# Order of transfers and weight splits around the start of an attention block: last weights sliced per head, first keys fetched in the third group, v of two heads split first

## The reference, cut to what matters

```
h = rms_norm(x)
c_q, c_kv, k_rope, z = split(h @ w_in)          # widths 768, 256, 32, 1024
q  = (rms_norm(c_q)  @ w_uq )  -> 16 heads x 96
kv = (rms_norm(c_kv) @ w_ukv)  -> 16 heads x (64 of k, 64 of v)
q, k = rope(rms_norm per head)
o = softmax(causal(q k^T / sqrt(96))) v
x = x + (o * silu(z)) @ w_out                   # the last product
```

## Time and profile before

| | us |
|---|---|
| three timed runs | 1054.29, 1054.57, 1055.83 |
| median | 1054.57 |
| the profiled execution | 1054.33 |
| its span | 1052.5 |
| PE busy | 1016.8 (97%) |
| PE weight loads busy | 845.5 (80%) |
| DVE busy | 611.9 (58%) |
| ACT busy | 464.8 (44%) |
| POOL busy | 226.8 (22%) |
| mean granted TensorE clock | 0.989 of full speed |

### The profile page before, as it was taken

The page is one execution under the profiler, slowest core; times in us unless marked ns, Lnnn a source line. Parts: engine busy times, 40 slices in busy tenths (PEclk is TensorE's granted clock), DMA queues, the critical chain, the costliest instruction groups (busy, mean ns, idle before and its releaser), DMA issues. The chain is left out here.

```text
span 1052.5 us, 15593 instructions
## 1 busy us (share of the span) xinstructions
PE 1016.8 (97%) x5979; PEld 845.5 (80%) x5979; DVE 611.9 (58%) x1111; ACT 464.8 (44%) x868; POOL 226.8 (22%) x397
## 2 busy tenths in 40 slices
PE   5999999999999999999999999998899999997998
PEld 4888888888888888888888999886677787776887
DVE  5653555436634443312453789977699999996221
ACT  6301111111223223322234766757699999997000
POOL 0000000000000002200001579884863333321000
PEclk9999999999999999999999999999899999998999
DMA  9300211211324332312102145485955444521222
GB/s 279 54 22 21 61 40 40 60 40 51 110 100 149 131 140 54 112 40 61 40 21 80 61 170 196 169 209 169 224 149 133 86 94 88 99 41 61 100 90 70
DMA packets 166427, 103.11 MB, mean 98 GB/s; under 512 B 76497, under 2 KB 150737, under 8 KB 166097
## 3 DMA queue, kind: packets, MB, share of 16 engines
q1 hardware_dynamic: 159280, 101.73, 34.3%
q10 hardware_dynamic: 7072, 0.39, 0.5%
HBM read 55.96 MB, written 29.36 MB: 81 GB/s over the span
## 5 line engine op out<-in xcount | busy, mean ns | idle before, releaser
L106 PE MATMUL banks<-front_act_hi,front_w_hi 128*128 128x512 f32 x608 | 239.9, 395 | 10.7 <-DVE front_w_lo L525 10.7
L108 PE MATMUL banks<-front_act_hi,front_w_lo 128*128 128x512 f32 x608 | 238.1, 392 | 0.0
L107 PE MATMUL banks<-front_act_lo,front_w_hi 128*128 128x512 f32 x608 | 237.9, 391 | 0.0
L106 PEld LDWEIGHTS banks<-front_act_hi,front_w_hi 128*128 128x128 f32 x608 | 115.1, 189 | 36.7 <-issue 8.7
L107 PEld LDWEIGHTS banks<-front_act_lo,front_w_hi 128*128 128x128 f32 x608 | 115.0, 189 | 24.2 <-issue 0.5
L108 PEld LDWEIGHTS banks<-front_act_hi,front_w_lo 128*128 128x128 f32 x608 | 114.9, 189 | 24.0
L374 POOL TENSOR_TENSOR front_sq<-front_sq,front_squares 128x1024 f32<-128x1024 f32 x6 | 14.4, 2397 | 450.5 <-ACT front_squares L487 450.5
L392 ACT ACTIVATE front_w_hi<-front_w 128x1024 fp32r<-128x1024 f32 x43 | 45.6, 1060 | 148.2 <-DMA front_w<-in_w_in_ab 103.1
L1418 DVE TENSOR_TENSOR heads_pt_lo<-banks,heads_pt_hi 128x512 f16<-128x512 f32 (+2 forms) x192 | 102.2, 554 | 14.1 <-ACT heads_pt_hi L1309 9.5
L1309 ACT ACTIVATE heads_pt_hi<-banks 128x512 f16<-128x512 f32 (+2 forms) x192 | 89.2, 486 | 18.7 <-PE banks L1577 18.6
L1595 PE MATMUL banks<-heads_v,heads_pt_hi 128*128 128x128 f16 x576 | 75.9, 222 | 2.8 <-POOL heads_v L1514 1.9
(11 more groups left out here) (246 smaller groups left out, 2070.5 us busy)
## 6 DMA issues: line engine op xcount, KB each, us to landing
qk_scratch<-heads_y SPq DMA_DIRECT2D x32, 512.0 KB, 3.3
front_w<-in_w_in_ab SPq DMA_DIRECT2D x21, 512.0 KB, 3.9
front_w<-in_w_in_c SPq DMA_DIRECT2D x17, 512.0 KB, 4.1
y<-in_x_t SPq DMA_DIRECT2D x8, 512.0 KB, 8.1
front_w<-in_w_out_ab SPq DMA_DIRECT2D x8, 512.0 KB, 4.0
front_x<-in_x_t SPq DMA_DIRECT2D x8, 512.0 KB, 5.2
x_scratch<-front_x SPq DMA_DIRECT2D x8, 512.0 KB, 4.0
v_scratch<-heads_v SPq DMA_DIRECT2D x32, 128.0 KB, 3.0
```

The source lines that it names most:

```text
L106: nc.tensor.matmul(out, w_hi, a_hi, start=first, stop=False)
L107: nc.tensor.matmul(out, w_hi, a_lo, start=False, stop=False)
L108: return nc.tensor.matmul(out, w_lo, a_hi, start=False, stop=last)
```

## The change

Four edits, none of which adds or removes arithmetic.

1. Table `when`: the splits of the next group's weights move from t = 2, 3, 4, 5, 6 with 3, 2, 1, 1, 1 chunks to t = 3, 4, 5, 6 with 1, 2, 2, 3.
2. Transposing loads of k and q are issued apart. k of head 0 is loaded in the third group (t = 1), q of head 0 there at t = 3; k and q of head 1 in the fourth group at t = 1 and t = 3, v of heads 0 and 1 at t = 5. The wait for group 0's stores moves to the third group, the wait for the end of group 2's products stays ahead of head 1's k.
3. The 8 slices of `w_out` are no longer issued in a row after the last unit. One goes behind the q and k of each head 4 to 11.
4. GpSimd splits v of head 1 directly behind that of head 0, ahead of `finish(28)`.

```diff
-    when = {2: chunks[0:3], 3: chunks[3:5], 4: chunks[5:6], 5: chunks[6:7], 6: chunks[7:8]}
+    when = {3: chunks[0:1], 4: chunks[1:3], 5: chunks[3:5], 6: chunks[5:8]}
...
-        def load_qk(h):
-            e, first = h % 2, slice(h * BLK, (h + 1) * BLK)
-            sp.dma_start_transpose(k_t[e][:], qk_d[:, 1, first]).then_inc(qk_in[e], 16)
-            sp.dma_start_transpose(q_t[e][:], qk_d[:, 0, first]).then_inc(qk_in[e], 16)
+        def load_k(h):
+            sp.dma_start_transpose(k_t[h % 2][:], qk_d[:, 1, h * BLK:(h + 1) * BLK]).then_inc(qk_in[h % 2], 16)
+
+        def load_q(h):
+            sp.dma_start_transpose(q_t[h % 2][:], qk_d[:, 0, h * BLK:(h + 1) * BLK]).then_inc(qk_in[h % 2], 16)
...
-            if t == 0 and g == G - 1:
+            if g == G - 2 and t == 1:
                 group_stored(0)
+                load_k(0)
+            if g == G - 2 and t == 3:
+                load_q(0)
+            if g == G - 1 and t == 1:
                 sp.wait_ge(q_ready, (G - 1) * NT)
-            if g == G - 1 and t in (0, 2):
-                load_qk(t // 2)
-            if g == G - 1 and t == 4:
+                load_k(1)
+            if g == G - 1 and t == 3:
+                load_q(1)
+            if g == G - 1 and t == 5:
                 load_v(0)
...
         sp.wait_ge(q_ready, UNITS)
-        for m in range(NK):
-            sp.dma_start(w_next[:, m], w_out.rearrange("(k p) c -> p k c", p=P)[:, :, m * P:(m + 1) * P]
-                         ).then_inc(w_next_in, 16)
         for h in range(2, HEADS):
             if h % HPG == 0:
                 group_stored(h // HPG)
             sp.wait_ge(s_ready, NT * (h - 1))
-            load_qk(h)
+            load_k(h)
+            load_q(h)
+            if 0 <= h - HPG < NK:
+                m = h - HPG
+                sp.dma_start(w_next[:, m], w_out.rearrange("(k p) c -> p k c", p=P)[:, :, m * P:(m + 1) * P]
+                             ).then_inc(w_next_in, 16)
             if h % 2 == 0:
                 sp.wait_ge(v_low, h)
                 load_v(h)
...
         split_v(0)
+        split_v(1)
         finish(LATE)
         for h in range(HEADS):
-            if h + 1 < HEADS:
+            if 1 < h + 1 < HEADS:
                 split_v(h + 1)
```

## The result

The changed kernel takes 1049.14 us in the median of five runs (1047.12 to 1051.10). Five runs of the kernel before beside them have a median of 1055.26. The ratio is 0.9941, with a 95% interval of 0.9924 to 0.9958: faster by 6.1 us. The forecast was 1044.8 with a range up to 1049.0, so the direction was right, the gain was 6.1 in place of 9.6, and the time fell just outside. The profiled execution took 1049.57, its span 1047.8, 4.7 less than before.

A forecast was written before the change was run, and what follows sets the result against it. TensorE, busy 97% of the span, bounds the kernel; only idle and low-clock stretches can yield time. Attention start 2.3 us plus heads 1 and 2 7.3 us, 9.6 off, gave 1044.8 us, own range 1043 to 1046.5, wider range 1041.2 to 1049.

The forecast's parts named there:

- v of head 1 first, head 2's q in time: Heads 1 and 2: TensorE's waits of 1.95 and 2.95 us go with their slow stretches, gaining 7.3 us.
- The bound of 15.5: Head 1: VectorE is busy 15.54 us in its window, so it can't come under 15.5 us.
- One sign: Heads 1 and 2: the granted clock between them was to be 1.00.
- the fourth rival: Heads 1 and 2: only one wait goes with its slow stretch, 3.3 us; 1051.1 us, chance 0.05.
- The slices, one per head: Heads 4 to 11: one w_out transfer behind each head's q delays no later load; cost taken as nothing.
- Head 1's k and q in the fourth group: Fourth group: with one pair of loads, the store goes out earlier and the attention's start moves up by 2.6 us.
- Head 0's k in the third group: Third group: its load behind the weights delays a store; ScalarE waits 0 to 4 us, TensorE 0 to 1.5.
- The second rival: Third group: k of head 0 delays a store and gives back the fourth group's gain; 1047.1 us, chance 0.15.
- The weight splits: Third group: first split at t = 3 removes ScalarE's 2.86 us landing wait; with head 0's loads, taken as -0.3 us.
- the sign of this: Third group: the forecast is wrong if TensorE waits over 2 us near 662 or near 678.
- The margin of 0.24 us: Splits at t = 6: the last ended at 679.50, TensorE read it at 679.74; zero to 0.6 us of waiting expected.
- The rule that I quoted: SyncE's queue: a transposing load behind a burst of weights waits for the burst, and the store behind it for both.

The follow-up runs named there:

- experiment 2: Kernel before with two edits alone, w_out sliced per head and v of head 1 split right behind that of head 0: 1045.23 us, ratio 0.9911.
- Experiment 8: Kernel before with v of head 1 split first, alone: 1055.16 us, ratio 1.0003.
- experiment 4: Kernel before with only the loads of k and q of heads 0 and 1 and of v moved as in the change: 1052.86 us, ratio 0.9982.
- experiment 1: Changed kernel with the old table of weight splits: 1044.06 us, ratio 0.9902 against the kernel before.
- experiment 3: Kernel before with the new table of weight splits alone: 1060.61 us, ratio 1.0050.
- experiment 6: Changed kernel, new table kept, each group's weights issued in parts of 2, 3 and 3 behind three units' stores, two units earlier: 1043.28 us, ratio 0.9897.
- experiment 7: Kernel before with w_out sliced per head alone: 1047.46 us, ratio 0.9934.

## Why the prediction was wrong, by its own steps

**v of head 1 first, head 2's q in time: right.** Neither wait is left. Head 1 takes 14.96 us (forecast 15.5), head 2 13.11. The gain is 7.86 against 7.3. The bound of 15.5 was a wrong reading. VectorE's 15.54 us were those of a window of 21.19 us, and some of that work was already head 2's: 15 low parts of the probabilities, where head 1's own window has 12, in the changed kernel as in experiment 2. The roots in it are the same in both.

```profile
L1418 DVE TENSOR_TENSOR heads_pt_lo<-banks,heads_pt_hi 128x512 f16<-128x512 f32 (+3 forms) x15 | 7.8, 545 | 3.0 <-ACT heads_pt_hi L1309 3.0
...
L1426 DVE TENSOR_TENSOR heads_pt_lo<-banks,heads_pt_hi 128x512 f16<-128x512 f32 (+3 forms) x12 | 6.3, 553 | 0.5 <-ACT heads_pt_hi L1317 0.2
```

VectorE is busy 13.63 us in head 1 now, and head 1 takes 14.69 in experiment 2. So the number came out near by some luck. One sign was missed: the clock between the two waits was to be 1.00, and it is 0.89 in head 1, where the slow stretch of the start now lies. Experiment 8 adds what the sum hid: the two edits don't add. v first is worth nothing while q is late, and the slices alone are worth 7.0, so the 3.3 us that the fourth rival gave to either wait alone fit neither.

**The slices, one per head: right.** There is no wait for q or k in heads 3 to 12, and the slices with v first give more alone (9.4 us) than the four edits together (6.1), with intervals that just overlap.

**Head 1's k and q in the fourth group: right in kind.** With the third group's loads and the old table the timed gain is 1.9 us (0.4 to 3.4), and the trace has 1.7 to head 0's first exponentials. 2.3 was forecast for the start; that the length shows just 2.3 is luck, as 0.6 of it is a slow stretch that fell elsewhere. `finish(24)` starts at 703.49 there, near the 703 forecast. In the changed kernel TensorE has no wait in the fourth group, ScalarE waits for no store there, and GpSimd is idle 1.39 us ahead of `finish(24)` in place of 3.19, but it starts it only at 709.20, after all that was lost before.

**Head 0's k in the third group: it cost nothing that experiment 4 could show**, at the low end of the 0 to 1.5 us that I gave it. k took 4.75 us of SyncE, inside the bounds, but the store that matters is issued ahead of it. The second rival was near in its number (1047.1) and wrong in its cause: the gain of the fourth group was given back, but by the splits.

**The weight splits: this step failed.** I wrote "With the first split at t = 3 that landing wait goes", and took half of VectorE's 2.0 us as time won. I had read the releaser of ScalarE's wait at 658.46 and not what stood behind it in ScalarE's list: the next y needs a store that is queued behind the same burst. Before, ScalarE waited 2.6 to 2.9 us for the weights, split three chunks in the time in which the store was still on its way, and had only 0.16 us to wait for its landing:

```profile
621.35 0.84 ACT L1294 ACTIVATE heads_y<-heads_x 128x768 f16<-128x768 f32 x1 [0.16 <-DMA qk_scratch<-heads_y]
```

In the third group y came 4.48 us after the end of the squares, with the splits between, and 4.41 in the changed kernel without them. The wait was not removable at that place; the splits in it were free. Moved out, the idle stretch grew to 5.90 us, and the splits came on top of a VectorE that was 20.98 of 24 us busy. The term was taken with the loads at -0.3 us; the table alone costs 4.1 us beside the other edits (experiment 1 against the result) and 5.3 by itself (experiment 3). In experiment 3's trace at least 1.5 us are the slow stretch in the third group, which no term of the sum had; the kernel of experiment 1 has one there too, so it is no part of the 4.1. The prediction named the sign of this, a wait of TensorE over 2 us near 662, and it came: 2.16 us, up to 665.42. Without this step the forecast would have been about right: experiment 1 differs from the changed kernel in the table alone and gained 10.3 us, against 9.6 forecast. I had also looked at the third group only. The table acts in the second as well, where TensorE's 1.39 us for a low part stands; I had bounded that wait at 0.6, with the end of VectorE's list moved up, and it moved down.

The margin of 0.24 us was a good warning, read too kindly. The rule that I quoted, from the Trainium skill, DMA: Bandwidth & Descriptors, section "Queues, rings and completion order", that each transfer engine consumes SyncE's transfers in ring order, spoke of the very thing. The traces agree with it in what they show: 7.5 us for a store behind the burst, 3.3 in the median. I applied it to the new load behind the burst and not to the store that had always stood there.

**What stays open.** The changed kernel's runs lie between 1047.1 and 1051.1 us, with a mean granted clock of 0.993 in the fastest and 0.990 in the slowest, and experiment 4's between 1050.0 and 1056.2. The same store behind the same burst is landed after 6.4 us in the kernel before and after 7.7 in experiment 1. What sets either was not tried. Nor was what part of the 5.3 us in experiment 3 is the longer landing and what the three splits at t = 6; experiment 6 only shows that the splits cost 0.4 us of waiting when ScalarE isn't stopped. And the waits of TensorE that a trace names do not add up to all that a delay costs: of the 4.0 us above some 0.7 lie in neither idle time nor the slow stretch.

## What to carry to other kernels

A wait on one transfer often covers the wait on the next transfer of the same queue. Before moving work out of a wait, look what the engine would wait for next: if that is queued behind the same burst, the wait stays, and the work in it was free. Ask of a burst which transfers with a waiter stand behind it, and put it where its waiters have slack: with the new table, two units earlier, whole or in parts, was worth 4 to 5 us. With the old table, whose splits filled the wait, the burst in parts and two units earlier gained 0.7 us, which is not clear of noise. And where two late inputs follow one another, as v and q here, mending the earlier one gains nothing until the later one is mended.

## What the runs showed of the hardware that I had not expected

The clock does not fall behind every stop of the same length. After the wait of 1.95 us for v, the granted clock was 0.50 for the next 2.7 us in the kernel before, and 1.94 us of the same wait in experiment 7 had no slow stretch behind it. The slow stretch that stood at 722 us before, right behind the 1.89 us, stands ten microseconds behind the 1.88 us in the changed kernel, with full clock between them (columns: us, busy, granted clock, share of the transfer engines, GB/s):

```profile
727.00:729.00 2.00, 2.00 (x28) 1.00 0.07 19
729.00:731.00 2.00, 2.00 (x28) 1.00 0.00 0
...
735.00:737.00 2.00, 2.00 (x7) 0.50 1.17 261
```

In experiment 4 even a wait of 3.01 us for head 2's q has full clock behind it (first line), and kernel 6 has full clock from the first projections to the end of head 2 (second line), with the same wait of 1.88 us at the start of the attention.

```profile
750.10:755.10 5.00, 5.00 (x44) 1.00 1.12 270
...
566.00:760.00 194.00, 187.81 (x1196) 1.00 0.53 154
```

After 6.9 us of standing still in experiment 8 the clock was 0.50 for at least 3.6 us. In the third group a wait of 2.16 us was followed by a slow stretch and one of 1.01 us by none. So in this kernel a stretch of some 3 us, which costs about 1.6, can't be put down to the length of one wait, and a forecast should carry it as a chance. It moves the time of a whole execution by as much as some of the edits here.
